# Merges of the first block: each head's sum of squares as one accumulating square on ScalarE, in place of one large square on GpSimd and three reductions on VectorE

## The chip, the cores and the metric

The kernel runs on 1 core of a Trainium2 chip. The metric is the device time of one execution in microseconds, given as the median of several runs. All tensors are fp32, and large products are made exact enough by splitting each operand into a high and a low part and multiplying three times.

## The reference

Two transformer-like blocks follow one another on 1024 tokens of width 1024. The first block has two layers. Each layer projects the normalised tokens, runs three branches (a gated linear attention of 4 heads of 64 values, a differential attention of 4 heads of 128 values, and an HGRN scan of 4 heads of 64 values), and merges them. The change is in the merge alone, which the reference writes so:

```python
def rms_norm(x, w):
    xf = x.astype(jnp.float32)
    xf = xf * lax.rsqrt(jnp.mean(xf * xf, axis=-1, keepdims=True) + EPS)
    return xf.astype(x.dtype) * w
...
    o = rms_norm(o, norm_w)                  # per head, in each of the three branches
    return merge_heads(o) * jax.nn.silu(g)   # g: gate values, one per element
...
        y = jnp.concatenate([y_a, y_b, y_c], axis=-1) @ w_out[layer]
        x = x + rms_norm(y, norm_post[layer])
```

So every token of every layer needs 12 sums of squares: 4 over 64 values, 4 over 128 and 4 over 64.

## The kernel before

The kernel is a sequence of stages with a barrier of all engines between groups of stages. The merge of a layer of the first block is the class `Merge1`. It runs twice, once for each layer, together with a small stage `Ahead` that starts the loads and the first weight split of the next projection.

`Merge1` handles the 1024 tokens as 8 tiles n = 0 to 7 of 128 tokens (the partitions) by 1024 values. For each tile:

- SyncE's queue fetches the branch outputs into `o` and the gates into `g`, in six transfers (L1252 to L1257), once tile n - 2 has been transposed.
- GpSimd squares the whole tile, `sq = o * o` (L1274), when the fetch has landed and the sums of the tile before have been taken from `sq`.
- VectorE sums `sq` by heads in three reductions (L1344: 4 heads of 64, 4 of 128, 4 of 64) and makes 12 means of them with two small operations (L1347, L1348). This is `dve_sums`.
- ScalarE forms the gate's logarithm with Abs, Exp and Ln over 1024 columns (L1418 to L1420), then the 12 reciprocal roots with Ln and Exp (L1422, L1423). This is `act_logs`.
- VectorE, in `dve_gate`: one subtraction for the sigmoid's exponent (L1353, waits for L1420), three products of `o` with the roots (L1358), the product with `g` (L1360, waits for the sigmoid of L1428 on ScalarE), and the product of both (L1362).
- TensorE transposes the gated tile with 8 transposes (L1439, called turn(n) below, waits for L1362). ScalarE copies it out of PSUM as the high part (L1411) and VectorE forms the low part (L1316).
- TensorE multiplies it with the output weights in 48 matmuls of 512 columns (L1457, called the product of n). ScalarE squares the product with an accumulated sum (L1389), VectorE makes the mean (L1298), ScalarE its root (L1394, L1395), and VectorE scales it and adds the residual x (L1304, L1306). ScalarE's queue stores the tile (L1400).

The order on every engine is written out by hand. In the loop, TensorE does turn(n + 1) and then the product of n. With m = n - 1, ScalarE does: square of product m, copy of tile n + 1, root of m, `act_logs(n + 2)`, store of m, sigmoid of n + 2. VectorE does: low part of n + 1, mean of m, `dve_sums(n + 2)`, scale and add of m, `dve_gate(n + 2)`. Tiles 0, 1 and 2 are gated before the loop; between them stand the eight splits of the output weights (L1334 on ScalarE, L1330 on VectorE).

Of the kernel before, what the change touches and what calls it, by code (L numbers as in the profile page):

```python
# [11 lines left out]
ALU = mybir.AluOpType  # L12
ACT = mybir.ActivationFunctionType
AX = mybir.AxisListType.X
# [3 lines left out]
NT = T // P  # L18
# [28 lines left out]
class Event:  # L47


    def __init__(self, sem, base, total, step, name):  # L50
        self.sem, self.base, self.total, self.step, self.name = sem, base, total, step, name
        self.given = 0
# [393 lines left out]
class Ahead(Stage):  # L446
# [38 lines left out]
    pool = pe  # L485


class Scan(Stage):
# [246 lines left out]
    @staticmethod  # L735
    def sides(x, l, first, side, step):

        half = 1 << l - 1
        return bass.AP(tensor=x.tensor, offset=x.offset + first, ap=[x.ap[0], [2 * half, 3 * P // (2 * half)], [side, 2], [step, half]])
# [119 lines left out]
    def pool(self):  # L859
        G, half = self.nc.gpsimd, lambda l: 1 << l - 1  # L860
        for n in range(NT):
            for l in range(1, LEVELS + 1):
                yield n * self.PERIOD + 11 + 2.15 * l
                if l == 1:
                    G.wait_ge(*self.summed(n))
                d, b, sides, h, g = self.space(n, l), self.b[:, 0], self.sides, half(l), LEVELS * n + l - 1 - self.SPACES
                if g >= 0:
                    G.wait_ge(*self.mixed(8 * (g // LEVELS) + g % LEVELS + 1))
                G.tensor_tensor(sides(d[:, 0], l, 0, h, 1), sides(b, l, h - 1, 3 * P + 1, 0), sides(b, l, 0, 3 * P + h, 1), ALU.subtract)  # L869
                G.tensor_tensor(sides(d[:, 1], l, 0, h, 1), sides(b, l, 3 * P, h - 3 * P, 1), sides(b, l, 3 * P + h, -3 * P - 1, 0),  # L870
                                ALU.subtract).then_inc(*self.spaced.inc())
# [61 lines left out]
class DiffPrepare(Stage):  # L933
# [60 lines left out]
    def pool(self):  # L994
        G = self.nc.gpsimd
        for n in range(NT):
# [222 lines left out]
class Merge1(Stage):  # L1219
# [4 lines left out]
    def __init__(self, k, layer, p1, o_scan, o_diff, src, xs, wo, consts):  # L1224
        super().__init__(k, f"merge1_{layer}")
        self.layer, self.p1, self.o_scan, self.o_diff, self.src, self.xs = layer, p1, o_scan, o_diff, src, xs
        t, sig = self.tile, self.event
        (self.raw, self.wl, self.wh), (self.hw, self.pw, self.dsc) = wo, consts
        self.o, self.g, self.x, self.sq = t("o", [P, 2, D]), t("g", [P, 2, D]), t("x", [P, 2, D]), t("sq", [P, D])
        self.ss, self.rs, self.e = t("ss", [P, 2, 16]), t("rs", [P, 2, 16]), t("e", [P, D])  # L1230
        self.yh, self.yl = t("yh", [P, 2, D], F32R), t("yl", [P, 2, D], F32R)
        self.y, self.ys = t("y", [P, 2, D]), t("ys", [P, 2])
        self.fetched = [sig("dma", f"fetched{s}", 3 * NT) for s in range(2)]
        self.x_loaded = [sig("dma", f"x_loaded{s}", NT // 2) for s in range(2)]
        self.stored = [sig("dma", f"stored{s}", NT // 2) for s in range(2)]
        self.o_squared = sig("pool", "o_squared", NT)
        self.summed, self.meant, self.logs, self.silu, self.gated, self.copied_v, self.y_meant, self.y_scaled, self.added = (
            sig("dve", x, NT) for x in ("summed", "meant", "logs", "silu", "gated", "copied_v", "y_meant", "y_scaled", "added"))
        self.logged, self.rstd, self.sigmoid, self.copied_s, self.y_squared, self.y_rstd = (
            sig("act", x, NT) for x in ("logged", "rstd", "sigmoid", "copied_s", "y_squared", "y_rstd"))  # L1240
        self.turned, self.projected = sig("pe", "turned", NT), sig("pe", "projected", NT)
        self.columns, self.high, self.low = sig("dve", "columns", 1), sig("act", "high", KT), sig("dve", "low", KT)

    def sp(self):
# [15 lines left out]
        for n in range(NT):  # L1260
# [3 lines left out]
                SP.wait_ge(*self.added(n - 2))  # L1264
            SP.dma_start(self.x[:, n % 2], self.src[n * P:(n + 1) * P, :]).then_inc(*self.x_loaded[n % 2].inc())
            yield n + 0.5

    def pool(self):
        G = self.nc.gpsimd
        for n in range(NT):  # L1270
            G.wait_ge(*self.fetched[n % 2](6 * (n // 2) + 5))
            if n:
                G.wait_ge(*self.summed(n - 1))
            G.tensor_tensor(self.sq[:], self.o[:, n % 2], self.o[:, n % 2], ALU.mult).then_inc(*self.o_squared.inc())  # L1274
            yield n - 2

    def dve(self):
        V = self.nc.vector
# [61 lines left out]
    def dve_sums(self, n):  # L1340
        V, c, s, ss = self.nc.vector, self.k.vo.chain, n % 2, self.ss
        V.wait_ge(*self.o_squared(n))
        for a, b, w, h in self.HEADS:
            last = V.reduce_sum(ss[:, s, h:h + (b - a) // w], self.heads(self.sq, a, b, w), axis=AX)  # L1344
        last.then_inc(*self.summed.inc())
        V.wait_ge(*self.summed(n))
        c(V.tensor_scalar(ss[:, s, 4:8], ss[:, s, 4:8], 0.5, None, ALU.mult))  # L1347
        V.tensor_scalar(ss[:, s, 0:12], ss[:, s, 0:12], 1.0 / 64, EPS, ALU.mult, ALU.add).then_inc(*self.meant.inc())  # L1348

# [63 lines left out]
    def act_logs(self, n):  # L1413
        S, c, e, s = self.nc.scalar, self.k.so.chain, self.e, n % 2
        S.wait_ge(*self.fetched[s](6 * (n // 2) + 5))
        if n:
            S.wait_ge(*self.gated(n - 1))
        c(S.activation(e[:], self.g[:, s], ACT.Abs))  # L1418
        c(S.activation(e[:], e[:], ACT.Exp, scale=-1.0))
        S.activation(e[:], e[:], ACT.Ln, bias=1.0).then_inc(*self.logged.inc())  # L1420
        S.wait_ge(*self.meant(n))
        c(S.activation(self.rs[:, s, 0:12], self.ss[:, s, 0:12], ACT.Ln))  # L1422
        S.activation(self.rs[:, s, 0:12], self.rs[:, s, 0:12], ACT.Exp, scale=-0.5).then_inc(*self.rstd.inc())  # L1423
# [1573 lines left out]
```

## Time and profile before

| | |
|---|---|
| median of 3 runs | 3813.46 us (3802.16 to 3821.61) |
| profiled execution, its own time | 3804.65 us |
| span of the trace | 3802.8 us |
| busy share of the span, TensorE matmul / VectorE / ScalarE / GpSimd | 82% / 56% / 35% / 15% |
| mean granted TensorE clock | 0.897 of full speed |
| the two merges | from about 880 to 1022 us, and from about 1917 to 2059 us |

The trace lists instructions by engine with start, duration, source line and tile. DVE is VectorE, ACT is ScalarE, POOL is GpSimd, PE is TensorE's matmul and PEld its weight load. A group in square brackets at the end of a row says how long the engine sat idle before and what released it. A row of the windows view gives a stretch and its length, then busy time and count of instructions for PE, PEld, DVE, ACT and POOL, and at the end the granted clock, the busy share of the DMA engines and their GB/s. A granted clock of 1.0 is 2.4 GHz, and 0.5 is 1.2 GHz.

### The profile page before, as it was taken

To read this page: it belongs to the slowest core of one execution; us is meant where nothing else is said; L and a number is where in the kernel's file an instruction comes from. 1 tells how busy PE (TensorE), PEld (TensorE's weight loads), DVE (VectorE), ACT (ScalarE), POOL (GpSimd) and SP (SyncE) were. 2 spreads that over 40 slices of the span, in tenths; PEclk is the share of its full clock that TensorE was granted. 3 is DMA by queue.
4 is the path that set the end of the run, shared out by engine and by line. 5 is a ranking of instruction groups with operands and counts; after the bars stand their busy time and mean duration, and the time that the engine had idled before them with its cause. 6 is when DMAs were issued, how large, how long until landed. Compare 5 with 4: busy or idle time off the path is not lost. (4 is left out here: it accounts for less than half of the span.)

```text
span 3802.8 us, 83247 instructions
## 1 busy us (share of the span) xinstructions
PE 3134.4 (82%) x36396; PEld 2654.8 (70%) x36396; DVE 2142.7 (56%) x3567; ACT 1341.1 (35%) x2390; POOL 578.6 (15%) x466
## 2 busy tenths in 40 slices
PE   7999986666899999645468998779999688886699
PEld 7988884444798888534357897777778577775344
DVE  3455447877625555479776365466676344553452
ACT  3133325644421333356443232234444122221541
POOL 0200004431002000145310011001000122221100
PEclk9999996767999999856589999899999699998899
DMA  3532213214435221131243344463331421112330
GB/s 126 173 98 79 79 39 97 79 48 164 151 101 184 80 79 47 55 74 48 81 163 127 138 153 146 160 187 112 110 103 61 116 48 40 45 40 70 144 108 34
DMA packets 268263, 378.79 MB, mean 100 GB/s; under 512 B 45173, under 2 KB 207277, under 8 KB 266552
## 3 DMA queue, kind: packets, MB, share of 16 engines
q1 hardware_dynamic: 165834, 260.49, 22.2%
q10 hardware_dynamic: 102066, 112.97, 8.6%
q8 instruction: 287, 4.70, 0.5%
q14 instruction: 76, 0.62, 0.1%
HBM read 256.42 MB, written 118.94 MB: 99 GB/s over the span
## 5 line engine op out<-in xcount | busy, mean ns | idle before, releaser
L385 PE MATMUL psum<-proj_w_low,h_high 128*128 128x344 f32 (+1 forms) x1984 | 668.9, 337 | 17.5 <-DVE proj_y L411 14.4
L385 PE MATMUL psum<-proj_w_high,h_high 128*128 128x344 f32 (+1 forms) x1984 | 658.0, 332 | 0.0
L385 PE MATMUL psum<-proj_w_high,h_low 128*128 128x344 f32 (+1 forms) x1984 | 657.1, 331 | 0.0
L385 PEld LDWEIGHTS psum<-proj_w_low,h_high 128*128 128x128 f32 x1984 | 376.8, 190 | 33.4 <-DVE proj_y L411 16.2
L385 PEld LDWEIGHTS psum<-proj_w_high,h_high 128*128 128x128 f32 x1984 | 376.7, 190 | 6.9
L385 PEld LDWEIGHTS psum<-proj_w_high,h_low 128*128 128x128 f32 x1984 | 376.3, 190 | 7.1
L385 PE MATMUL psum<-proj_rest_w_low,h_high 128*128 128x304 f32 x640 | 207.7, 325 | 34.2 <-DVE proj_rest_w_low L400 22.6
L869 POOL TENSOR_TENSOR scan_d<-scan_b 128x384 f32<-128x384 f32 x112 | 124.2, 1109 | 622.5 <-DVE scan_b L710 608.6
L411 DVE COPY proj_y<-psum 128x344 f32<-128x344 f32 (+1 forms) x130 | 70.3, 541 | 243.7 <-PE psum L385 235.2
L1169 DVE COPY diff_wt<-psum 128x512 f32<-128x512 f32 x64 | 44.3, 692 | 282.6 <-PE psum L1115 282.6
L385 PE MATMUL psum<-proj_rest_w_high,h_low 128*128 128x304 f32 x640 | 194.6, 304 | 0.0
L385 PE MATMUL psum<-proj_rest_w_high,h_high 128*128 128x304 f32 x640 | 194.5, 304 | 0.0
L1147 DVE TENSOR_REDUCE diff_nm<-psum 128x1 f32<-128x1024 f32 x128 | 156.3, 1221 | 12.6 <-PE psum L1092 12.0
L437 ACT ACTIVATE proj_y<-psum 128x344 f32<-128x344 f32 (+1 forms) x130 | 62.0, 477 | 269.1 <-PE psum L385 257.5
L385 PEld LDWEIGHTS psum<-proj_rest_w_low,h_high 128*128 128x128 f32 x640 | 122.3, 191 | 46.0 <-DVE proj_rest_w_low L400 23.0
L1102 PEld LDWEIGHTS psum<-diff_v,diff_wt 128*128 128x128 f32 x1024 | 119.1, 191 | 49.8 <-issue 44.7
L1188 ACT ACTIVATE diff_w<-psum,diff_nm 128x1024 f32<-128x1024 f32 x128 | 141.3, 1110 | 27.9 <-DVE diff_nm L1148 23.8
L1092 PE MATMUL psum<-diff_kk,diff_q 64*128 64x512 f32 x512 | 130.3, 628 | 9.9 <-DMA diff_v<-proj 9.9
L2364 PE MATMUL psum<-delta_xt,delta_ym 64*64 64x32 f32 x3200 | 118.3, 218 | 21.9 <-issue 21.8
L1102 PE MATMUL psum<-diff_v,diff_wt 128*128 128x128 f32 x1024 | 131.2, 281 | 3.5 <-DVE diff_wt L1169 3.5
L870 POOL TENSOR_TENSOR scan_d<-scan_b 128x384 f32<-128x384 f32 x112 | 130.4, 1164 | 0.0
L2364 PEld LDWEIGHTS psum<-delta_xt,delta_ym 64*64 64x64 f32 x3200 | 111.0, 138 | 19.6 <-issue 19.5
(416 smaller groups left out, 6954.7 us busy)
## 6 DMA issues: line engine op xcount, KB each, us to landing
proj_raw<-in_w_in SPq DMA_DIRECT2D x24, 1376.0 KB, 6.6
proj<-proj_y ACTq DMA_DIRECT2D x192, 172.0 KB, 1.8
delta_x<-dn_qkv SPq DMA_DIRECT2D x40, 384.0 KB, 5.2
proj<-proj_y ACTq DMA_DIRECT2D x68, 224.0 KB, 1.9
dn_prep_x<-proj SPq DMA_DIRECT2D x54, 256.0 KB
proj_raw<-in_w_in SPq DMA_DIRECT2D x7, 1792.0 KB, 9.3
modulate_w<-in_mod_w SPq DMA_DIRECT2D x16, 768.0 KB, 4.6
merge_z<-proj SPq DMA_DIRECT2D x8, 1536.0 KB, 7.2
```

Of the source, the lines that this page charges most:

```text
L385: last = PE.matmul(self.ps[:, j % self.banks, 0:self.width], hp[:, kt, tokens], wp[:, c % 2, kt, :], start=kt == 0 and n == 0, stop=kt == ...
L411: V.tensor_copy(self.y[:, j % 4, :], self.ps[:, j % self.banks, 0:self.width]).then_inc(*self.copied[1].inc())
L437: S.activation(self.y[:, j % 4, :], self.ps[:, j % self.banks, 0:self.width], ACT.Copy).then_inc(*self.copied[0].inc())
L869: G.tensor_tensor(sides(d[:, 0], l, 0, h, 1), sides(b, l, h - 1, 3 * P + 1, 0), sides(b, l, 0, 3 * P + h, 1), ALU.subtract)
L870: G.tensor_tensor(sides(d[:, 1], l, 0, h, 1), sides(b, l, 3 * P, h - 3 * P, 1), sides(b, l, 3 * P + h, -3 * P - 1, 0), ALU.subtract).then_ ...
L1092: last = PE.matmul(ps[:, self.bank + 2 * cc + half, :], self.q[rows, s, t * P:(t + 1) * P], self.kk[rows, s, half * 512:(half + 1) * 512], ...
L1102: last = PE.matmul(self.out(), self.wt[:, z, j * P:(j + 1) * P], self.v[:, s, j, :], start=j == 0, stop=j == 7)
L1147: c(V.reduce_max(nm[:, z, cc:cc + 1], self.both(cc), axis=AX))
L1169: V.tensor_copy(self.wt[:, z, 512:1024], self.ps[:, self.bank + 5]).then_inc(*self.copied_v.inc())
L1188: S.activation(self.w[:, z, cc], self.both(cc), ACT.Exp, bias=self.nm[:, z, cc:cc + 1], scale=0.125, accum_out=self.sm[:, z, cc:cc + 1]).t ...
L2364: return self.nc.tensor.matmul(out, left, right, start=start, stop=stop, tile_position=(64 * i, 64 * o))
```

## The change

The square on GpSimd, the three reductions on VectorE and the signal `summed` between them go. In `act_logs`, ahead of Abs, ScalarE issues 12 Square activations, one for each head, each with an accumulated sum that is written straight into the head's column of `ss`. The last one gives the signal `o_squared`, which VectorE's two small operations (L1347, L1348) wait for. The `sq` tile is still written, by the squares.

```diff
-        self.o_squared = sig("pool", "o_squared", NT)
+        self.o_squared = sig("act", "o_squared", NT)
...
-    def pool(self):
-        G = self.nc.gpsimd
-        for n in range(NT):
-            G.wait_ge(*self.fetched[n % 2](6 * (n // 2) + 5))
-            if n:
-                G.wait_ge(*self.summed(n - 1))
-            G.tensor_tensor(self.sq[:], self.o[:, n % 2], self.o[:, n % 2], ALU.mult).then_inc(*self.o_squared.inc())
-            yield n - 2
...
     def dve_sums(self, n):
         V, c, s, ss = self.nc.vector, self.k.vo.chain, n % 2, self.ss
         V.wait_ge(*self.o_squared(n))
-        for a, b, w, h in self.HEADS:
-            last = V.reduce_sum(ss[:, s, h:h + (b - a) // w], self.heads(self.sq, a, b, w), axis=AX)
-        last.then_inc(*self.summed.inc())
-        V.wait_ge(*self.summed(n))
...
         S.wait_ge(*self.fetched[s](6 * (n // 2) + 5))
         if n:
             S.wait_ge(*self.gated(n - 1))
+        for a, b, w, h in self.HEADS:
+            for i in range((b - a) // w):
+                cols = slice(a + w * i, a + w * (i + 1))
+                last = S.activation(self.sq[:, cols], self.o[:, s, cols], ACT.Square, accum_out=self.ss[:, s, h + i:h + i + 1])
+        last.then_inc(*self.o_squared.inc())
         c(S.activation(e[:], self.g[:, s], ACT.Abs))
```

## Rows read from the trace of the kernel before

**Rows 1.** Busy time by engine in the first merge (windows view).
```profile
879.90:1022.00 142.10, 104.76 (x448) 83.89 (x448) 106.75 (x134) 69.94 (x105) 18.09 (x8) 0.86 0.44 146
```

**Rows 2.** Turns on TensorE, layer 0 and layer 1 (timeline of PE).
```profile
922.74 1.97 PE L1439 MATMUL psum<-ident,merge_o 128*128 128x128 f32 x8 [6.47 <-DVE merge_o L1362]
...
966.35 1.09 PE L1439 MATMUL psum<-ident,merge_o 128*128 128x128 f32 x8 [2.00 <-DVE merge_o L1362]
...
980.59 1.09 PE L1439 MATMUL psum<-ident,merge_o 128*128 128x128 f32 x8 [1.99 <-DVE merge_o L1362]
...
994.23 1.04 PE L1439 MATMUL psum<-ident,merge_o 128*128 128x128 f32 x8
...
2016.97 1.09 PE L1439 MATMUL psum<-ident,merge_o 128*128 128x128 f32 x8 [2.04 <-DVE merge_o L1362]
...
2031.52 1.09 PE L1439 MATMUL psum<-ident,merge_o 128*128 128x128 f32 x8 [2.33 <-DVE merge_o L1362]
```

**Rows 3.** VectorE in one period of the loop (timeline of DVE).
```profile
968.64 1.23 DVE L1316 TENSOR_TENSOR merge_yl<-psum,merge_yh 128x1024 fp32r<-128x1024 f32 x1 [2.34 <-ACT merge_yh L1411]
...
969.84 1.33 DVE L1344 TENSOR_REDUCE merge_ss<-merge_sq 128x4 f32<-128x256 f32 x3
...
973.96 2.92 DVE L1353 SCALAR_TENSOR_TENSOR merge_e<-merge_g,merge_e 128x1024 f32<-128x1024 f32 x1
...
979.31 1.23 DVE L1362 TENSOR_TENSOR merge_o<-merge_o,merge_e 128x1024 f32<-128x1024 f32 x1
```

**Rows 4.** ScalarE in the same period: Abs and Ln (timeline of ACT).
```profile
970.30 1.04 ACT L1418 ACTIVATE merge_e<-merge_g 128x1024 f32<-128x1024 f32 x1
...
972.47 1.06 ACT L1420 ACTIVATE merge_e<-merge_e 128x1024 f32<-128x1024 f32 x1
```

**Rows 5.** GpSimd in the same period (timeline of POOL).
```profile
972.85 2.94 POOL L1274 TENSOR_TENSOR merge_sq<-merge_o 128x1024 f32<-128x1024 f32 x1 [11.31 <-DMA merge_g<-proj]
```

**Rows 6.** VectorE's gate in the next period, no square on GpSimd (timeline of DVE).
```profile
988.70 1.22 DVE L1353 SCALAR_TENSOR_TENSOR merge_e<-merge_g,merge_e 128x1024 f32<-128x1024 f32 x1
...
992.36 1.22 DVE L1362 TENSOR_TENSOR merge_o<-merge_o,merge_e 128x1024 f32<-128x1024 f32 x1
```

**Rows 7.** ScalarE with an accumulated sum, and a 256-column operation (timeline of ACT).
```profile
1503.43 1.11 ACT L1188 ACTIVATE diff_w<-psum,diff_nm 128x1024 f32<-128x1024 f32 x1
...
1504.43 0.20 ACT L1188 ACTIVATION_READ_ACCUMULATOR diff_w<-psum,diff_nm 128x1 f32 x1
1504.52 1.11 ACT L1188 ACTIVATE diff_w<-psum,diff_nm 128x1024 f32<-128x1024 f32 x1
...
647.68 0.40 ACT L795 ACTIVATE scan_f<-scan_lt 128x256 f32<-128x256 f32 x1
```

**Rows 8.** Gating of tiles 0, 1 and 2 before the loop (timelines of ACT and DVE).
```profile
886.95 1.06 ACT L1418 ACTIVATE merge_e<-merge_g 128x1024 f32<-128x1024 f32 x1 [2.40 <-DMA merge_g<-proj]
...
892.24 1.21 DVE L1353 SCALAR_TENSOR_TENSOR merge_e<-merge_g,merge_e 128x1024 f32<-128x1024 f32 x1
...
907.80 1.83 DVE L1348 TENSOR_SCALAR merge_ss<-merge_ss 128x12 f32<-128x12 f32 x1
...
914.53 1.06 ACT L1418 ACTIVATE merge_e<-merge_g 128x1024 f32<-128x1024 f32 x1 [2.66 <-DVE merge_o L1362]
...
917.79 1.23 DVE L1353 SCALAR_TENSOR_TENSOR merge_e<-merge_g,merge_e 128x1024 f32<-128x1024 f32 x1 [1.70 <-ACT merge_e L1420]
```

**Rows 9.** ScalarE: Abs of tile 7 (985.04, 2022.92), squares of two products (ACT).
```profile
937.18 1.02 ACT L1389 ACTIVATE merge_y<-psum 128x1024 f32<-128x1024 f32 x1 [1.95 <-PE psum L1457]
...
985.04 1.04 ACT L1418 ACTIVATE merge_e<-merge_g 128x1024 f32<-128x1024 f32 x1
...
1006.45 1.03 ACT L1389 ACTIVATE merge_y<-psum 128x1024 f32<-128x1024 f32 x1 [3.20 <-PE psum L1457]
...
2022.92 1.04 ACT L1418 ACTIVATE merge_e<-merge_g 128x1024 f32<-128x1024 f32 x1
```

**Rows 10.** Granted clock just after the turn at 922.74 (windows view).
```profile
922.70:927.00 4.30, 4.26 (x14) 3.75 (x15) 2.22 (x2) 1.02 (x1) 1.74 (x1) 0.50 0.29 77
```

More of the change, by code:

```diff
@@ L1235, in __init__ @@
         self.stored = [sig("dma", f"stored{s}", NT // 2) for s in range(2)]
-        self.o_squared = sig("pool", "o_squared", NT)
-        self.summed, self.meant, self.logs, self.silu, self.gated, self.copied_v, self.y_meant, self.y_scaled, self.added = (
-            sig("dve", x, NT) for x in ("summed", "meant", "logs", "silu", "gated", "copied_v", "y_meant", "y_scaled", "added"))
+        self.o_squared = sig("act", "o_squared", NT)
+        self.meant, self.logs, self.silu, self.gated, self.copied_v, self.y_meant, self.y_scaled, self.added = (
+            sig("dve", x, NT) for x in ("meant", "logs", "silu", "gated", "copied_v", "y_meant", "y_scaled", "added"))
         self.logged, self.rstd, self.sigmoid, self.copied_s, self.y_squared, self.y_rstd = (
```

## Prediction

> **What bounds the kernel now.** I read the page first: the merges of the first block are two stretches of about 142 us in a span of 3802.8 us, so only some 7% of the time can move at all. The windows view of the first merge [rows 1] shows no engine full: TensorE 104.8 us and VectorE 106.8 us of 142.1, ScalarE 69.9, GpSimd 18.1. With no full engine the limit is a loop through several of them, and the timelines of the loop show which. A turn starts at 966.35 and the next at 980.59, a period of 14.24 us, and each of them had TensorE idle for 2.0 us waiting for VectorE's last gating product [rows 2]. From one turn to the next, VectorE is the chain: low part of the tile at 968.64 (2.29 us after the turn began, after ScalarE's copy), sums at 969.84, then means, scale and add, gate from 973.96, last product from 979.31 [rows 3], and the turn 1.28 us after that. ScalarE runs beside it: Abs at 970.30, Ln ended at 972.47 + 1.06 = 973.53 [rows 4], 0.43 us before VectorE took the result. The reader should see two things there: ScalarE is only 0.4 us from being the bound, and TensorE has 2.0 us of slack in 14.24.
>
> One more thing is in these rows. L1353 lasted 2.92 us [rows 3], while GpSimd's square ran from 972.85 for 2.94 us [rows 5]; one period later, with no square beside it, the same operation lasted 1.22 us [rows 6]. So the square costs VectorE 1.70 us by running beside it. Seven of the sixteen L1353 look like this, and one L1358.
>
> **The change part by part.** Below, S is the start of a turn, and offsets are from S.
>
> *Removed from VectorE:* three reductions, 1.33 us [rows 3], plus the 1.70 us of contention. That is 3.03 us of the 14.24 us chain in most periods. *Removed from GpSimd:* its square; nothing else waits for GpSimd here.
>
> *Added to ScalarE:* 12 squares and 12 accumulator reads in a row. The trace has no such small accumulating square, so I build it. A 1024-column operation lasts 1.04 us [rows 4] and a 256-column one 0.40 us [rows 7]: 0.833 ns a column on top of 0.19 us, so 0.24 us for 64 columns and 0.29 us for 128. An accumulator read starts 0.11 us before the end of its operation (1503.43 + 1.11 against 1504.43), and the next operation starts 0.09 us after the read began although the read lasts 0.20 us [rows 7]. Operation and read together thus take up 1.09 us where the operation alone lasts 1.11, so a pair costs about its operation's duration: 8 x 0.24 + 4 x 0.29 = 3.1 us, less 12 x 0.01 to 0.02, 3.0 us. Bounds: if the reads hid wholly, each operation would cost its duration less 0.10 and the twelve 2.0 us (2.1 - 0.1); if small operations and reads didn't overlap at all, 3.1 + 12 x 0.20 = 5.5 us. I take 3.0, since both overlaps are seen in the same row pair.
>
> The Trainium skill (ScalarE: Activation LUTs, What ACT_TABLE_LOAD costs) gives an ACTIVATE with immediate operands 186 ns + 0.833 ns a column, says that neighbours overlap by about 93 ns, and prices no accumulator read. By it alone the twelve squares would take 2.0 us and the total below would be about +3 us. The rows of L1188 show that the read does take its 0.09 us turn.
>
> *Where these 3.0 us lie.* They are issued in `act_logs`, behind the root of the product before and in front of Abs. Behind them on ScalarE are queued Abs, Exp, Ln, the 12 roots and the sigmoid; VectorE's gate waits for Ln, and VectorE's scale and add stand behind its wait for the squares. In a usual period Abs would start at 970.30 - 966.35 = 3.95 [rows 2, 4]. Now the squares stand there, Abs starts at 6.95, and Ln ends 3.23 later at 10.18 (972.47 + 1.06 - 970.30 = 3.23 [rows 4]). VectorE gets the sums at 7.0. From the end of the reductions to the start of L1353, with the means, the scale and the add between, it needed 973.96 - 969.84 - 1.33 = 2.8 us [rows 3], so it is ready at 9.9 and waits for Ln. L1353 starts at 10.20. From L1353 to L1362 takes 992.36 - 988.70 = 3.66 without contention [rows 6], and 1.28 more to the turn (980.59 - 979.31 [rows 2, 3]). The next turn is at 15.14, against 14.24: **+0.90 us a period**. The saving on VectorE, 3.03 us, is all spent: ScalarE becomes the longer arm of the loop.
>
> *All tiles.* Tile 0: from Abs at 886.95 to L1353 at 892.24 was 5.29 us [rows 8]; now 3.0 + 3.23 + 0.02 = 6.25, +0.95. Tile 1 is covered: VectorE's splits of the weights end later than the squares, and it saves there. Tile 2: L1353 at 917.79 waited for ScalarE, whose Abs at 914.53 waited for tile 1's gate [rows 8]. Tile 1's gate comes 2.05 us earlier (0.95 for the shift, less 1.33 for the reductions and about 1.7 for L1348, a tiny operation that lasted 1.83 beside GpSimd's square [rows 8]), and the squares put 3.0 in front of Abs: again +0.95 in all, not twice. Four periods from turn 2 to turn 6, all taken as the usual one: 4 x 0.90 = +3.6. From turn 6 to turn 7 there is no contention to win back and the weight split of `Ahead` lies in the way: Abs at 985.04 - 980.59 = 4.45 [rows 2, 9], so the turn at 4.45 + 3.0 + 3.23 + 0.02 + 3.66 + 1.28 = 15.64 against 994.23 - 980.59 = 13.64 [rows 2], +2.0. Layer 0: 0.95 + 3.6 + 2.0 = 6.55 us. Layer 1: the same 0.95 + 3.6, then Abs at 2022.92 - 2016.97 = 5.95, so 17.14 against 2031.52 - 2016.97 = 14.55, +2.6 [rows 2, 9]: 7.15 us. Together **+13.7 us**.
>
> *The clock.* TensorE's idle time before a turn grows from 2.0 to about 3.0 us, and before turn 7 to 3.5 us in layer 0 and 5.0 us in layer 1 (period less 12.1 us of its work). After 6.47 idle the turn at 922.74 took 1.97 us and the granted clock was 0.50 (1.2 GHz) for the 4.3 us that follow; after 2.0 idle the turns took 1.09 [rows 2, 10]. From turn to finished product it was 937.18 - 922.74 = 14.44 us there and 1006.45 - 994.23 = 12.22 at full clock [rows 2, 9]: 2.2 us. Behind turn 7 TensorE is the bound, so this would count in full. I take it in layer 1 and half of it in layer 0: **+3.3 us**. In the loop, where 14.4 us still fit into a period of 15.1, only the slow transposes would count, and I take them at nothing.
>
> The fetches, the residual loads and the stores are hidden as before: the fetch that a turn releases had landed 6.5 us after it (972.85 - 966.35 [rows 2, 5]) and is needed a whole period later than the turn. Stores move some 2 us later, and nothing waits for them within that. Square runs between Ln and Exp today (L1389) without a table load.
>
> Sum: +17.0 us, or 3804.65 + 17.0 = 3821.7 against the profiled execution's own time. That execution was 8.8 us under the median of its kernel (3813.46), so for a median I add the change to the median: 3830.5 us, +0.45%. About 0.5% (19 us) is what a measurement of this kernel can tell from no change, so the forecast lies just inside.
>
> **The rivals.**
>
> *The small pairs don't overlap* (12 squares at 5.5 us): 2.5 us more in eight places of each layer, the five periods and all three tiles before them, since VectorE's splits then no longer cover tile 1. That is 16 x 2.5 = 40 us more, 3870.5 us. For it: no row shows an operation as short as the read that follows it. Against: rows 7. Chance 0.10.
>
> *The clock falls at each turn.* The slow transposes delay ScalarE's copy by 0.88 us (1.97 against 1.09 [rows 2]). At eight more turns (3 to 6 of both layers), and with the full 2.2 us in layer 0, this is 7 + 1 = 8 us more: 3838.5 us. For it: idle time grows from 2.0 to 3.0 us, and nothing in the rows lies between 2.3 and 6.5 us. Against: after 2.3 us the turn was fast. Chance 0.17. The Trainium skill (TensorE: Matmul & The Clock Gate, Why this matters for your kernels) advises against idle gaps between bursts of matmuls, since the clock falls behind them; by that rule this rival is what happens, and the rows so far can't exclude it.
>
> *The contention isn't GpSimd's* but the transfers', so that L1353 still takes 2.92 us: 1.7 us more in eight periods, 3844 us. For it: a square starts when a fetch has landed, so both are near. Against: the long operation ends with the square [rows 3, 5], and without a square it is short [rows 6]. Chance 0.05.
>
> *The reads are hidden* (2.0 us for all twelve): 1.0 us less in the five periods and in tiles 0 and 2 of each layer, 14 us less, 3817 us. Chance 0.09.
>
> *Faster:* ScalarE does the squares in time in which it idled, and VectorE's 3.03 us come through until TensorE is the bound at 12.1 us a tile. This needs the squares to delay Abs by under 0.4 us. Then eight periods give 2.1 us each, tile 0 some 2 us in each layer, the last periods some 4 together: 25 us less, 3788 us. For it: ScalarE idles half of the merge [rows 1]. Against: its order is written out, and its idle time lies behind the sigmoid and the roots, not ahead of Abs. Chance 0.04.
>
> **How the numbers follow.** The forecast has 0.55. Its own range is +8 to +26 us with the runs' scatter, and about four tenths of it lies above 19 us. Slower by over 0.5%: 0.22 of the forecast, 0.10 of unlapped pairs, 0.12 of the clock, 0.04 of the contention, 0.48 in all, less a hundredth for scatter. Within 0.5%: 0.33 + 0.05 + 0.01 + 0.09 = 0.48. Faster: 0.04, and a hundredth for scatter. The range for 8 in 10 leaves out the unlapped pairs above and the faster case below: 3812 to 3846 us, which takes in the clock and the contention.
>
> **What would show it.** In the changed kernel's timeline: twelve squares and reads of about 3.0 us in front of Abs; L1353 at 1.2 us everywhere and waiting for L1420 rather than started by VectorE's own order; turns 15.1 us apart with 3 us idle before them; 15.6 and 17.1 us before turn 7; turn 7 of layer 1 at half clock; no GpSimd in the merge; the other stages of equal length. Wrong would be: the squares at 2 or 5.5 us, turns of 1.97 us throughout, or VectorE still the engine that ends last in the loop.

## The result and the profile after

The changed kernel takes 3828.98 us, the kernel before 3810.57 us (medians of 20 runs each). The ratio is 1.0053, with a 95% interval of 1.0036 to 1.0070: slower by half a percent, or some 20 us. The forecast was 3830.5 us against a median before of 3813.46, +0.45%, so the time and the direction came out as forecast, on the edge between "no change" and "slower". The change itself was forecast at 17.0 us and measured at 18.4.

In the profiled executions the span grew by 21.1 us, from 3802.8 to 3823.9. The two merges account for 19.3 of it. Measured from the first operation on the head weights to the start of the last residual add, they took 140.7 and 141.2 us before (sum 281.9), and take 149.8 and 151.4 us now (sum 301.2). This sum is the yardstick for the experiments, since it is free of the scatter elsewhere in the span; each sum comes from one profiled execution. The ends of the second merge after, in VectorE's timeline:

```profile
1924.46 0.21 DVE L1270 TENSOR_SCALAR heads_w<-heads_w,diff_scale 128x1 f32<-128x1 f32 x1 [2.38 <-PEq L179]
...
2075.85 1.23 DVE L1297 TENSOR_TENSOR merge_y<-merge_y,merge_x 128x1024 f32<-128x1024 f32 x1
```

The windows view of the first merge after the change, to be set beside [rows 1] (the stretch is 8 us longer, as the merge is):

```profile
879.90:1030.00 150.10, 107.72 (x448) 86.03 (x448) 85.47 (x109) 94.27 (x297) 0.00 (x0) 0.85 0.42 138
```

VectorE went from 106.8 to 85.5 us, GpSimd from 18.1 to nothing, ScalarE from 69.9 to 94.3 (where a square and its accumulator read overlap, the time counts once). The sum of busy time over the three engines fell by 15 us, and the stage became longer. What counts is seen in one period of the loop. ScalarE after, from the copy of a tile to the sigmoid (the squares left out are like those shown, four of them over 128 columns):

```profile
941.05 1.03 ACT L1398 ACTIVATE merge_yh<-psum 128x1024 fp32r<-128x1024 f32 x1 [1.95 <-PE psum L1431]
943.53 0.20 ACT L1381 ACTIVATE merge_ys<-merge_ys 128x1 f32<-128x1 f32 x1 [1.45 <-DVE merge_ys L1289]
943.76 0.20 ACT L1382 ACTIVATE merge_ys<-merge_ys 128x1 f32<-128x1 f32 x1
943.87 0.24 ACT L1408 ACTIVATE merge_sq<-merge_o 128x64 f32<-128x64 f32 x1
944.02 0.19 ACT L1408 ACTIVATION_READ_ACCUMULATOR merge_sq<-merge_o 128x1 f32 x1
944.11 0.24 ACT L1408 ACTIVATE merge_sq<-merge_o 128x64 f32<-128x64 f32 x1
...
946.96 1.05 ACT L1410 ACTIVATE merge_e<-merge_g 128x1024 f32<-128x1024 f32 x1
948.04 1.06 ACT L1411 ACTIVATE merge_e<-merge_e 128x1024 f32<-128x1024 f32 x1
949.13 1.06 ACT L1412 ACTIVATE merge_e<-merge_e 128x1024 f32<-128x1024 f32 x1
...
951.49 1.06 ACT L1420 ACTIVATE merge_e<-merge_e 128x1024 f32<-128x1024 f32 x1 [0.95 <-DVE merge_e L1340]
```

And VectorE in the same period:

```profile
943.35 0.14 DVE L1289 TENSOR_SCALAR merge_ys<-merge_ys 128x1 f32<-128x1 f32 x1
947.09 0.17 DVE L1334 TENSOR_SCALAR merge_ss<-merge_ss 128x4 f32<-128x4 f32 x1 [3.59 <-ACT merge_sq L1408]
...
950.23 1.23 DVE L1340 SCALAR_TENSOR_TENSOR merge_e<-merge_g,merge_e 128x1024 f32<-128x1024 f32 x1 [0.31 <-ACT merge_e L1412]
```

The reader should see that the squares start at 943.87 and Abs at 946.96, which is 7.04 us after the turn at 939.92, that VectorE sits idle 3.59 us until the last square, and that its gate then waits for ScalarE once more. Before, VectorE took the same stretch without an idle gap [rows 3]. L1340 (L1353 before) took 1.22 to 1.23 us in all sixteen tiles, where seven took 2.92. The turns on TensorE, to be set beside [rows 2]:

```profile
939.92 1.10 PE L1431 MATMUL psum<-ident,merge_o 128*128 128x128 f32 x8 [1.97 <-DVE merge_o L1349]
...
955.18 1.96 PE L1431 MATMUL psum<-ident,merge_o 128*128 128x128 f32 x8 [3.01 <-DVE merge_o L1349]
...
971.29 1.09 PE L1431 MATMUL psum<-ident,merge_o 128*128 128x128 f32 x8 [2.26 <-DVE merge_o L1349]
...
986.54 1.09 PE L1431 MATMUL psum<-ident,merge_o 128*128 128x128 f32 x8 [1.44 <-DVE merge_o L1349]
...
1002.28 1.32 PE L1431 MATMUL psum<-ident,merge_o 128*128 128x128 f32 x8 [3.50 <-DVE merge_o L1349]
...
2048.01 1.97 PE L1431 MATMUL psum<-ident,merge_o 128*128 128x128 f32 x8 [5.03 <-DVE merge_o L1349]
```

From 939.92 to 955.18 is a usual period, 15.26 us. From 955.18 to 971.29 is 16.11 us, because the turn itself ran at about half clock (1.96 us). The windows view of the 3 us from each of these two turns on:

```profile
955.18:958.18 3.00, 3.00 (x11) 2.75 (x12) 0.00 (x0) 1.00 (x1) 0.00 (x0) 0.51 1.06 389
971.29:974.29 3.00, 3.00 (x13) 2.53 (x14) 0.71 (x1) 1.02 (x1) 0.00 (x0) 0.67 0.49 160
```

The granted clock was 0.51 behind the slow turn, and 0.67 behind the fast one at 971.29. There it fell only after the turn was done. The longer product then ate idle time, of which 1.44 us is left before the turn at 986.54, and the period stayed at 15.25 us.

### The profile page after: what moved, and what is told of

Its sections match the earlier page's. It is cut to its first block and busy times, and to the rows that moved or that the text cites. A ratio compares the mean times of both kernels' runs of the same rounds, so it can differ in the third digit from the quotient of the medians.

```text
span 3823.9 us, 83553 instructions
## 1 busy us (share of the span) xinstructions
PE 3148.1 (82%) x36396; PEld 2666.1 (70%) x36396; DVE 2105.7 (55%) x3519; ACT 1390.3 (36%) x2774; POOL 541.9 (14%) x450
## 5 line engine op out<-in xcount | busy, mean ns | idle before, releaser
L2356 PE MATMUL psum<-delta_xt,delta_ym 64*64 64x32 f32 x3200 | 120.2, 220 | 18.6 <-issue 18.4
L2356 PEld LDWEIGHTS psum<-delta_xt,delta_ym 64*64 64x64 f32 x3200 | 113.1, 140 | 17.7 <-issue 17.5
```

The source lines that it names most:

```text
L2356: return self.nc.tensor.matmul(out, left, right, start=start, stop=stop, tile_position=(64 * i, 64 * o))
```

## The experiments

For each kernel the period is that of the usual turns in the first merge, and the sum is that of both merges. Ratios are to the kernel before, measured on the same chip.

| kernel | period us | sum us | ratio (95% interval) |
|---|---|---|---|
| before | 14.24 | 281.9 | 1 |
| changed | 15.25 | 301.2 | 1.0053 (1.0036 to 1.0070) |
| squares in front of the root | 13.68 | 273.6 | 0.9977 (0.9954 to 1.0000) |
| squares a tile ahead | 12.37 | 275.4 | 0.9981 (0.9960 to 1.0003) |
| before, GpSimd's square cut | 12.55 | 264.4 | 0.9952 (0.9927 to 0.9978) |
| one wide square in front of Abs | 14.10 | 282.4 | 0.9976 (0.9956 to 0.9996) |
| squares twice | 19.36 | 356.7 | 1.0199 (1.0158 to 1.0239) |
| no accumulator reads | 14.14 | 286.2 | 1.0015 (0.9998 to 1.0031) |
| busier TensorE | 15.25 | 301.4 | 1.0068 (1.0045 to 1.0091) |
| a tile ahead, tile 7 in front of the root | 12.37 | 266.5 | 0.9964 (0.9941 to 0.9987) |
| one wide square in front of the root | 12.55 | 265.6 | 0.9948 (0.9924 to 0.9972) |

**Squares twice.** Is the place of the squares the one that sets the end?

```diff
+        for again in range(2):
-        for a, b, w, h in self.HEADS:
+            for a, b, w, h in self.HEADS:
                 ...
+            if not again:
+                self.k.so.chain(last)
```

> Changed kernel with the twelve squares issued twice, the second set behind the end of the first. My theory: 3.2 us more in front of Abs in five periods and in the tiles before the loop, so turns 18.4 us apart and the merges 45 to 51 us longer, about 350 us; ratio to before 1.018. Rival (ScalarE's squares are not what sets the end): 301 us.

The turns, in TensorE's timeline:

```profile
951.84 1.97 PE L1434 MATMUL psum<-ident,merge_o 128*128 128x128 f32 x8 [5.76 <-DVE merge_o L1349]
971.19 1.97 PE L1434 MATMUL psum<-ident,merge_o 128*128 128x128 f32 x8 [5.29 <-DVE merge_o L1349]
```

The period grew by 4.11 us: 3.2 us for the second set, and 0.88 us because every turn of the loop now ran slowly, behind 4.7 to 5.8 us of idle time. The sum grew by 55.5 us, against 45 to 51 expected; slow turns, which the expectation left out, account for most of the difference. ScalarE's squares are on the path one for one.

**No accumulator reads.** What does a read cost?

```diff
-                last = S.activation(..., ACT.Square, accum_out=self.ss[:, s, h + i:h + i + 1])
+                kept = {"accum_out": self.ss[:, s, h + i:h + i + 1]} if n < 2 else {}
+                last = S.activation(..., ACT.Square, **kept)
```

> Changed kernel with squares of tiles 2 to 7 without an accumulated sum (the means are then made of old values: this leaves out part of the computation). It prices the accumulator reads. Theory: a square of 64 columns then follows the one before after 0.15 us instead of 0.24, the twelve take 2.0 us instead of 3.1, turns 14.2 us apart, merges about 289 us. Rival (reads are hidden, so nothing is won): 3.1 us and 301 us.

ScalarE's timeline merges the twelve squares into one row:

```profile
942.80 2.07 ACT L1409 ACTIVATE merge_sq<-merge_o 128x64 f32<-128x64 f32 x12
944.78 1.04 ACT L1411 ACTIVATE merge_e<-merge_g 128x1024 f32<-128x1024 f32 x1
```

From the first square to Abs is 1.98 us, with the reads 3.09: a read costs 0.093 us of the 0.19 that it lasts. This agrees with the overlap that the Trainium skill gives for neighbouring operations (ScalarE: Activation LUTs, What ACT_TABLE_LOAD costs), read here as holding for accumulator reads too. The period fell by 1.11 us.

**GpSimd's square cut in the kernel before.** Was the contention GpSimd's?

```diff
-            G.tensor_tensor(self.sq[:], self.o[:, n % 2], self.o[:, n % 2], ALU.mult)...
+            cols = slice(0, D if n == 0 else 8)
+            G.tensor_tensor(self.sq[:, cols], self.o[:, n % 2, cols], self.o[:, n % 2, cols], ALU.mult)...
```

> Kernel before, but from tile 1 on GpSimd squares only 8 columns, so that the sums are taken of mostly old squares (this leaves out part of the computation). VectorE's work is unchanged. My theory: L1353 takes 1.22 us in every tile and the merges shrink by about 1.7 us in ten places, to 262 us; ratio 0.995. Rival (the long operations come from transfers): L1353 still 2.92 us in seven tiles and 282 us.

VectorE's gate and the turns:

```profile
955.22 1.22 DVE L1354 SCALAR_TENSOR_TENSOR merge_e<-merge_g,merge_e 128x1024 f32<-128x1024 f32 x1
```

```profile
960.16 1.09 PE L1440 MATMUL psum<-ident,merge_o 128*128 128x128 f32 x8 [0.31 <-DVE merge_o L1363]
972.71 1.09 PE L1440 MATMUL psum<-ident,merge_o 128*128 128x128 f32 x8 [0.31 <-DVE merge_o L1363]
```

The operation took 1.22 to 1.23 us in all sixteen tiles, the period fell by 1.69 us, and the sum by 17.5. The transfers were untouched, so the 1.7 us are GpSimd's. The rows of before show more: the two engines took turns. GpSimd's square, 1.89 us at its shortest, took 2.36 to 2.94 us in these seven tiles, since it began beside VectorE's residual add. And VectorE's operation ended 1.08 to 1.09 us after the square's end in all seven (976.88 against 975.79 in [rows 3, 5]), however long the square had taken. Cutting the square is worth 17.5 us of 281.9, with VectorE's three reductions left in place, and TensorE is now only 0.3 us from being the bound.

**One wide square in front of Abs.** Half of the change: ScalarE squares, VectorE still sums.

```diff
-        for a, b, w, h in self.HEADS: ... (the twelve squares)
+        if n:
+            S.wait_ge(*self.summed(n - 1))
+        S.activation(self.sq[:], self.o[:, s], ACT.Square).then_inc(*self.o_squared.inc())
```

The diff is against the changed kernel; VectorE's three reductions and their signal `summed` are back as before.

> Half of the change: ScalarE forms the squares of a whole tile in one operation in front of Abs, without accumulated sums, and VectorE keeps its three reductions. My theory: Abs is delayed by 1.0 us, VectorE wins back 1.7 us of contention and then waits for the square; turns about 14.1 us apart, the merges 280 us, ratio 1.000. Rival (any work moved in front of Abs costs its full duration): 282 + 14 x 1.0 = 296 us.

VectorE's timeline, the first reduction and the gate:

```profile
950.87 1.34 DVE L1335 TENSOR_REDUCE merge_ss<-merge_sq 128x4 f32<-128x256 f32 x3 [1.46 <-ACT merge_sq L1411]
...
955.00 1.22 DVE L1344 SCALAR_TENSOR_TENSOR merge_e<-merge_g,merge_e 128x1024 f32<-128x1024 f32 x1
```

The period was 14.10 us as worked out, and the sum 282.4, nearly that of before (281.9). That is 1.55 us above the 12.55 of the kernel with GpSimd's square cut, and here it isn't the delay of Abs that costs them: the gate doesn't wait for ScalarE, but the reductions wait 1.46 us for the wide square. The ratio of 0.9976 is a little better than the merges explain; they are 0.5 us longer than before's in the trace.

**Squares in front of the product's root.** The same twelve squares, another place.

```diff
             if n + 1 < NT:
                 self.act_copy(n + 1)
+            if n and n + 2 < NT:
+                self.act_squares(n + 2)
             if n:
                 S.wait_ge(*self.y_meant(m))
```

Here `act_squares` holds the wait for the fetch and the twelve squares of the changed kernel. It doesn't wait for the gate of the tile before, as they do in `act_logs`. It is also called for tiles 0, 1 and 2 before the loop, each time in front of `act_logs`.

> Changed kernel with the twelve squares moved, in the loop, from behind the product's root to in front of it, between the copy of tile n + 1 and the wait for the mean, where ScalarE idled 1.45 us. My theory (the squares cost what they delay Abs): in the loop the turns come 13.7 us apart instead of 15.25, five periods a layer, so the two merges together take about 286 us instead of the 301.2 of the changed kernel and the 281.9 of the kernel before; ratio to before about 1.001. Rival (the amount of work on ScalarE counts, not its place): 301 us, ratio 1.005.

The turn on TensorE, then ScalarE's timeline, the copy, the first square, and the root, which in the changed kernel's rows above had an idle gap of 1.45 us before it:

```profile
945.10 1.09 PE L1439 MATMUL psum<-ident,merge_o 128*128 128x128 f32 x8 [1.43 <-DVE merge_o L1349]
```

```profile
946.23 1.03 ACT L1402 ACTIVATE merge_yh<-psum 128x1024 fp32r<-128x1024 f32 x1 [1.41 <-PE psum L1439]
947.15 0.25 ACT L1410 ACTIVATE merge_sq<-merge_o 128x64 f32<-128x64 f32 x1
...
950.23 0.19 ACT L1385 ACTIVATE merge_ys<-merge_ys 128x1 f32<-128x1 f32 x1
...
950.56 1.05 ACT L1418 ACTIVATE merge_e<-merge_g 128x1024 f32<-128x1024 f32 x1
```

Abs starts 5.46 us after the turn instead of 7.04. The same work delays it by 1.6 us less, and the period is 13.68, as worked out. The sum is 273.6, not 286. I had counted the loop alone: before the loop, tile 2's squares now run while ScalarE waits for tile 1's gate, where they had cost about 3 us in each layer, and no turn of the usual periods was slow.

**Squares a tile ahead**, behind the sigmoid. The main lines of the edit (tile 3's squares stand in front of a root, those of tiles 0 to 2 before the loop):

```diff
             if n and n + 2 < NT:
                 self.act_sigmoid(n + 2)
+            if n and n + 3 < NT:
+                self.act_squares(n + 3)
```

> Changed kernel with the squares of tile n + 3 issued behind the sigmoid of tile n + 2, where ScalarE idled before the next turn; tile 3's stand between a copy and a root. My theory: VectorE's 3.0 us come through, turns 12.6 us apart in the loop, the merges together about 270 us, ratio to before about 0.997. Rival (TensorE at 12.1 us a tile, or the later copy and square of the product, eat it): periods over 14 us, merges 282 us or more, ratio 1.000 or more.

TensorE's turns, and ScalarE at tile 7 (the last square of one tile, then the weight split, then the square of the product and the copy):

```profile
943.19 1.09 PE L1443 MATMUL psum<-ident,merge_o 128*128 128x128 f32 x8
955.56 1.09 PE L1443 MATMUL psum<-ident,merge_o 128*128 128x128 f32 x8
```

```profile
968.04 0.24 ACT L1414 ACTIVATE merge_sq<-merge_o 128x64 f32<-128x64 f32 x1
968.28 2.49 ACT L426 ACTIVATE proj_w_high<-proj_raw 128x2752 fp32r<-128x2752 f32 x1
970.68 1.00 ACT L1380 ACTIVATE merge_y<-psum 128x1024 f32<-128x1024 f32 x1
971.67 1.01 ACT L1406 ACTIVATE merge_yh<-psum 128x1024 fp32r<-128x1024 f32 x1
```

These turns have no idle time before them at all: TensorE is the bound, at 12.37 us. Yet the sum was 275.4, because at tile 7 the squares, the weight split and the product's square stand in a row on ScalarE and the copy of tile 6, turned at 967.93, comes only at 971.67.

**A tile ahead, but tile 7 in front of the root.** The two places combined; tile 7's squares leave the place behind the sigmoid.

> Like the kernel with the squares behind the sigmoid of the tile before (turns 12.4 us apart), but tile 7's squares stand between copy and root, so that they don't meet the weight split of the next projection on ScalarE. My theory: the last two copy periods of layer 0 fall from 14.8 + 13.1 to about 12.4 + 13.7, layer 1 wins about as much, the merges take about 271 us; ratio to before 0.997. Rival (TensorE's clock or its product, not ScalarE's queue, made those periods long): 275 us.

The copy periods of layer 0 at the end were 12.15 and 13.68 us where they had been 14.76 and 13.07, and the sum fell to 266.5, by more than expected. The order on ScalarE made those periods long. But that is only half of the 8.9 us. Layer 1's last turn, here and with all squares a tile ahead, and the stretch behind each:

```profile
2004.29 1.09 PE L1443 MATMUL psum<-ident,merge_o 128*128 128x128 f32 x8 [1.95 <-DVE merge_o L1349]
2004.29:2011.00 6.71, 6.71 (x33) 5.62 (x34) 3.79 (x4) 1.43 (x3) 0.00 (x0) 1.00 0.00 0
```

```profile
2016.66 1.97 PE L1443 MATMUL psum<-ident,merge_o 128*128 128x128 f32 x8 [5.04 <-DVE merge_o L1349]
2016.66:2023.00 6.34, 6.34 (x20) 5.35 (x21) 2.64 (x4) 1.43 (x3) 0.00 (x0) 0.53 0.00 0
```

The granted clock stayed at 1.00 behind turn 7, where it had been 0.53 (and 0.73 in layer 0). From turn 7 to the last residual add the two layers took 53.0 us instead of 57.4, which is the other half. The interval, 0.9941 to 0.9987, lies under 1.

**One wide square in front of the root.** Both lessons together: GpSimd's square goes from the kernel before, and VectorE keeps its three reductions. In the loop:

```diff
+            if n and n + 2 < NT:
+                self.act_squares(n + 2)      # here: one Square over 1024 columns, no accumulated sum
             if n:
                 S.wait_ge(*self.y_meant(m))
```

> One square of a whole tile on ScalarE in the 1.45 us in which it waits for the mean between copy and root; VectorE keeps its three reductions; tile 2's square stands behind tile 1's sigmoid. If what counts is VectorE's contention and what ScalarE has in front of Abs, this has neither: turns 12.55 us apart as with no GpSimd square at all, the merges about 265 us, ratio to before 0.995. If the square in the gap delays the root: 13.6 us apart and 275 us.

```profile
939.87 1.02 ACT L1408 ACTIVATE merge_yh<-psum 128x1024 fp32r<-128x1024 f32 x1
940.78 1.06 ACT L1415 ACTIVATE merge_sq<-merge_o 128x1024 f32<-128x1024 f32 x1
942.34 0.20 ACT L1391 ACTIVATE merge_ys<-merge_ys 128x1 f32<-128x1 f32 x1 [0.50 <-DVE merge_ys L1289]
```

The wide square fits into the gap with 0.50 us left, Abs isn't delayed, VectorE is undisturbed, and the period is 12.55 us, the same as with hardly any square at all. The sum is 265.6 us and the ratio 0.9948 (0.9924 to 0.9972): 3796.53 us against 3813.43 for the kernel before on that chip.

**A busier TensorE.** Does the idle time before a turn cause the slow turns, and how much of the loss is theirs?

```diff
-            PE.wait_ge(*self.gated(n))
             if n >= 2:
                 PE.wait_ge(*self.copied_v(n - 2))
+                for j in range(10):
+                    PE.transpose(ps[:, 4 * s + j % 2, 0:P], self.ident[:], self.ident[:])
+            PE.wait_ge(*self.gated(n))
```

> Changed kernel with ten more transposes of the identity on TensorE before each turn from turn 2 on, into the bank that the turn then overwrites, which fill about 1.3 us of its idle time of 3.0. Theory of the clock: turns of 1.97 us vanish from the loop, and the two merges shrink by the 4 us that slow turns and slow products cost, to 297 us. If the clock plays no part in the loss: 301 us.

```profile
947.93 1.25 PE L1430 MATMUL psum<-ident 128*128 128x128 f32 x10
951.10 1.92 PE L1433 MATMUL psum<-ident,merge_o 128*128 128x128 f32 x8 [1.92 <-DVE merge_o L1349]
...
967.18 1.09 PE L1433 MATMUL psum<-ident,merge_o 128*128 128x128 f32 x8 [1.14 <-DVE merge_o L1349]
```

The idle stretch before the turn was cut from 3.0 to 1.92 us, and the same turn of layer 0 was slow as in the changed kernel. In layer 1 the slow turn of the loop was gone (three periods of 15.26 us in a row, where one had been 15.99). Turn 7 of layer 1 still met the half clock, behind 3.96 us (granted 0.53 in the 5.2 us from its start). The sum didn't move (301.4 against 301.2). So the 4 us that I expected back didn't come, and one slow turn of two stayed behind a shorter idle stretch: the run leaves the cause of slow turns open.

## Why the prediction was right

**The bound and the limit of what can move.** Right. 19.3 us of the 21.1 us of span lie in the two merges. The other 1.8 us lie outside, and such differences between single executions are within their scatter.

**What is removed.** Right: 3.03 us a period of VectorE's chain are gone. The 1.70 us of contention are shown by cutting GpSimd's square alone (1.69 us a period); the 1.33 us of reductions came off VectorE's rows.

**What is added.** 3.0 us was forecast for twelve pairs, 3.09 measured, with 0.24 us and 0.29 us for a pair of 64 and 128 columns. The bounds of 2.0 and 5.5 are settled: reads hidden (2.0) and no overlap (5.5) were both wrong, and leaving the reads out gave 1.98.

**Where it lies.** Right, and the centre of the matter. The squares stand in front of Abs, and the period became 15.25 where 15.14 was forecast; the 0.09 us of the squares make most of the difference. Moving them 1.45 us of idle time earlier gave 1.57 us a period, and doubling them cost their length.

**Tile by tile.** In layer 0, turn 2 came 0.5 us later than before, counted from the merge's start (0.95 forecast; here the fetch landed 0.6 us earlier), turns 2 to 6 took 4.9 us more (3.6 forecast: 4 x 0.11 for the length of the period and 0.87 for the slow turn), turn 6 to 7 2.1 us more (2.0), the tail 1.6 more (1.1). In layer 1: 1.6 (with a fetch that landed 0.5 later), 4.5, 2.7 (2.6 forecast) and 1.4 (2.2). Together 19.3 against 17.0: the forecast was short by 2.3 us, nearly all of it slow turns in the loop and the 0.1 us a period. The times agree better than that, 3830.5 forecast and 3828.98 measured, and there luck helps: the median of the kernel before came down by 2.9 us with more runs.

**The clock.** The term of 3.3 us for the last turns measured 1.6 + 1.4 = 3.0. But it was distributed otherwise (1.1 and 2.2 forecast), so that the good sum is in part luck: layer 1's slow turn lasted 1.97 us, while layer 0's took 1.32 and its product was slow behind it. The rival with a slow turn at every tile didn't happen. A slow turn in each layer's loop did, which I had priced at nothing. They were the only two turns of the loops before turn 7 with 3.0 us of idle time in front (3.01 and 3.05); at the others a slow turn or a slow product before them had left 1.4 to 2.3 us. That these follow from more idle time is not shown: the busier TensorE had one of them too, behind 1.92 us.

The prediction read too few turns here. It holds that a turn was fast after 2.3 us of idle time and that no row lies between 2.3 and 6.5. The kernel before has a turn in layer 1's loop, behind 2.04 us, at which the clock fell; the turn, and the granted clock from its start on:

```profile
1988.23 1.34 PE L1439 MATMUL psum<-ident,merge_o 128*128 128x128 f32 x8 [2.04 <-DVE merge_o L1362]
1988.23:1990.50 2.27, 2.27 (x11) 2.08 (x12) 0.00 (x0) 0.89 (x1) 0.00 (x0) 0.66 1.05 391
```

It cost 0.26 us (a period of 14.50 us). So the clock fell in the loop before the change too.

**The chances.** I put 0.47 on slower by over 0.5% and 0.48 on less, and the measured +0.53% falls just beyond the line, with an interval that holds the line. Which of the two it would be was a toss-up, then and now. The rivals of contention by transfers, of hidden reads and of pairs without overlap are excluded by the runs. The rival on the faster side named the right condition: the same squares in ScalarE's idle time make the kernel faster than before, at best by 15 us in the merges (ratio 0.9964) where the rival had 25.

**Still open.** What makes a turn slow after 2 to 3 us of idle time. The length of the idle stretch alone doesn't say: behind 1.95 us the granted clock stayed at 1.00 (the turn at 2004.29 with tile 7 in front of the root), and behind 1.92 us the turn ran at about half clock (951.10 with the busier TensorE). No run varied one idle stretch by itself. Also, a ratio of 0.9977 for squares in front of the root, with 8.3 us won in the merges (0.2%), agrees with the trace but doesn't clear 1 by itself.

## What to carry to other kernels

Count the work that an edit puts in front of each operation that the other engine waits for, not the busy time of the engine that it relieves. ScalarE was idle half of the time, but its idle time lay elsewhere in its order; against the kernel before, the change was worth +19 us in the merges with the twelve squares in one place and -8 us with the same squares in another. And look for an operation that lasts longer than its twins when another engine works beside it: nearly the whole gain was to be had there (16 us of the 17.5 that cutting GpSimd's square gave), by a plain square in a gap that the trace already showed.

## What the runs showed of the hardware

- An accumulator read lasts 0.19 us and takes 0.093 us of ScalarE's time between short squares too: 12 pairs in 3.09 us against 12 plain squares in 1.98.
- A VectorE operation over two SBUF operands of 1024 columns took 2.92 us instead of 1.22 beside a GpSimd product of two SBUF operands, and 1.22 to 1.23 in all sixteen tiles once that product was cut to 8 columns. The two took turns: in all seven cases it ended 1.08 to 1.09 us after the product did, and the product took 2.36 to 2.94 us instead of 1.89.
- Eight transposes took 1.97 us behind 4.7 us or more of idle time in the turns of the doubled squares and of the changed kernel. Between 1.9 and 3.5 us both happened: 1.96 us behind 3.01 (changed kernel), 1.97 behind 2.40 (no accumulator reads) and 1.92 behind 1.92 us (busier TensorE), but 1.10 us behind 1.97, 1.09 behind 2.26 (changed kernel) and 1.09 behind 3.44 us (squares a tile ahead). The clock can also fall right behind a fast turn (0.67 in the 3 us from 971.29 on, in the changed kernel).
